# Attention scores as three fp32r passes over high and low parts, in a two-layer encoder kernel

## The reference

```python
q = partial_rope(_rms_f32(q, g_q), cos, sin) * (D_HD ** -0.5)
k = partial_rope(_rms_f32(k, g_k), cos, sin)
...
def block(qblk):                       # 128 queries
    s = jnp.einsum("bhcqd,bhckd->bhcqk", qblk, k)      # c: 2 components, d: 64
    p = jax.nn.softmax(s, axis=-1)
    a = p[:, :, 0] - lam * p[:, :, 1]
    return jnp.einsum("bhqk,bhkv->bhqv", a, v)
```

## Time and profile before

| | us |
|---|---|
| median of 3 runs | 1906.34 |
| lowest, highest | 1904.99, 1906.96 |
| the profiled execution | 1907.49 |
| its span, first to last instruction | 1905.7 |

### The profile page before, as it was taken

The page is one execution under the profiler, slowest core; times in us unless marked ns, Lnnn a source line. Parts: engine busy times, 40 slices in busy tenths (PEclk is TensorE's granted clock), DMA queues, the critical chain, the costliest instruction groups (busy, mean ns, idle before and its releaser), DMA issues.

```text
span 1905.7 us, 31585 instructions
## 1 busy us (share of the span) xinstructions
PE 1879.5 (99%) x10881; PEld 1750.2 (92%) x10881; DVE 1251.1 (66%) x2148; ACT 870.3 (46%) x1839; POOL 1159.5 (61%) x1533
## 2 busy tenths in 40 slices
PE   8999999999999999999999999999999999999999
PEld 7888887899999999999988888888889999999998
DVE  7756465677757665656776666666488575757673
ACT  5333333346444444444534444444465454544453
POOL 3533524357777868788863333333458787887885
PEclk9999999999999999999999999999999999999999
DMA  5559999527569898784366666655124435353534
GB/s 164 177 196 262 227 256 243 142 83 174 128 173 257 233 263 270 229 266 148 117 135 128 127 122 126 127 116 115 58 85 121 133 111 150 97 153 103 153 115 129
DMA packets 378986, 305.39 MB, mean 160 GB/s; under 512 B 14260, under 2 KB 322263, under 8 KB 378599
## 3 DMA queue, kind: packets, MB, share of 16 engines
q1 hardware_dynamic: 348304, 233.69, 40.3%
q0 software_dynamic: 28416, 69.21, 20.1%
q10 hardware_dynamic: 2134, 0.82, 0.2%
HBM read 298.88 MB, written 143.20 MB: 232 GB/s over the span
## 4 chain that ended last, share of the span: by engine, by line
PE 89%; DVE 6%; DMA 2%; ACT 1%; issue 1%; POOL 1%; DVEq 0%; SPq 0%; ACTq 0%; POOLq 0%
PE ps L929 48%; PE ps L836 26%; PE ps L1082 3%; PE ps L1243 3%; PE ps L1211 2%; PE ps L1062 1%; PE ps L1233 1%; PE ps L1145 1%; DMA raw<-in_sums 1%; DMA raw<-in_ffn_w_out_dram 1%; DVE gt L1586 1%; DVE rstd L1429 1%; PE ps L1091 1%; DVE sx L1481 0%; PE ps L1175 0%
## 5 line engine op out<-in xcount | busy, mean ns | idle before, releaser
L929 PE MATMUL ps<-sx,wh 128*128 128x400 f32 (+1 forms) x2044 | 532.3, 342 | 5.1 <-ACT gt L2163 4.2
L760 POOL TENSOR_TENSOR wl<-raw,wh 128x256 fp32r<-128x256 f32 (+1 forms) x432 | 356.4, 860 | 97.8 <-ACT wh L2148 96.5
L726 POOL CAST wh<-raw 128x256 fp32r<-128x256 f32 x248 | 102.2, 454 | 490.3 <-PE ps L836 466.5
L929 PEld LDWEIGHTS ps<-sx,wh 128*128 128x128 f32 x2044 | 374.5, 189 | 7.7 <-ACT gt L2163 5.3
L929 PE MATMUL ps<-sx,wl 128*128 128x400 f32 (+1 forms) x1022 | 348.5, 341 | 0.0
L760 POOL TENSOR_TENSOR wl<-raws,wh 128x256 fp32r<-128x256 f32 x328 | 282.3, 903 | 92.3 <-ACT wh L2148 92.0
L1640 DVE TENSOR_TENSOR h<-h,ps 128x400 f32<-128x400 f32 (+1 forms) x280 | 154.6, 559 | 131.9 <-PE ps L929 131.8
L929 PE MATMUL ps<-fx,wh 128*128 128x400 f32 (+1 forms) x904 | 235.2, 341 | 0.3 <-issue 0.2
L836 PE MATMUL ps<-xh,wh 128*128 128x512 f32 (+1 forms) x752 | 215.6, 363 | 0.0
L836 PE MATMUL ps<-xl,wh 128*128 128x512 f32 (+1 forms) x752 | 207.4, 349 | 0.0
L836 PE MATMUL ps<-xh,wl 128*128 128x512 f32 (+1 forms) x752 | 201.3, 345 | 0.0
(11 more groups left out here) (311 smaller groups left out, 3597.3 us busy)
## 6 DMA issues: line engine op xcount, KB each, us to landing
in_sums<-in_ffn_w_in_dram SPq DMA_DIRECT2D x16, 1536.0 KB, 9.3
raw<-in_sums SPq DMA_DIRECT2D x96, 256.0 KB, 3.1
in_sums<-in_ffn_w_in_dram SPq DMA_DIRECT2D x16, 1280.0 KB, 9.6
raw<-in_ffn_w_in_dram SPq DMA_DIRECT2D x80, 256.0 KB, 3.0
raws<-in_sums SPq DMA_DIRECT2D x80, 256.0 KB, 3.0
raw<-out_sums SPq DMA_DIRECT2D x120, 128.0 KB, 2.3
raws<-in_ffn_w_in_dram SPq DMA_DIRECT2D x52, 256.0 KB, 3.3
raw<-in_m_w_in_dram SPq DMA_DIRECT2D x24, 512.0 KB, 4.6
```

What stands on the lines that cost most here:

```text
L726: ins = pool.tensor_copy(wh[:, slot, c], raw[:, slot, c])
L760: ins = pool.tensor_tensor(slot_of(n, 1)[:, c], raw_of(n)[:, c], slot_of(n, 0)[:, c].bitcast(F32), ALU.subtract)
L929: mm = pe.matmul(product_bank(layer, s, j), slot_of(n, low_w)[:, k * P:(k + 1) * P], x, start=(j in OPENS and k + q == 0), stop=(k == tile ...
```

## The change

High and low parts of queries and keys are made, and each score matmul becomes three fp32r ones. The parts need room: the high rows lie in the four tiles of h that rest (`LATE`), which are stored to DRAM before attention and read back in the last head; the low rows lie over the first four rows of wk. `kd` becomes two, `kdh` and `kdl`.

```diff
+        def q_high(odd):
+            return high_rows[:, LATE[2 * odd], 0:TQ]
+        def k_high(odd):
+            return high_rows[:, LATE[2 * odd + 1], :]
+        def q_low(odd):
+            return low_rows[:, odd, 0:TQ]
+        def k_low(odd):
+            return low_rows[:, 2 + odd, :]
...
 SP, loads of the attention blocks n:
                 weights(MIX1 + n, n % 2, attn_cols(n % 3, (n // 3) * P))
+                if n == 1:
+                    sp.wait_ge(out_read, N_OUT)
+                    for odd in range(2):
+                        sp.dma_start(h_late[odd], h[:, LATE[2 * odd]:LATE[2 * odd] + 2, :]).then_inc(h_late_stored, 16)
+            def late_tiles_back(odd):
+                sp.wait_ge(sc_ready, (D_HEADS - 1 + odd) * NQ)
+                sp.wait_ge(h_late_stored, 32)
+                sp.dma_start(h[:, LATE[2 * odd]:LATE[2 * odd] + 2, :], h_late[odd]).then_inc(h_late_back[odd], 16)
...
 POOL:
+            def query_lows(g):
+                odd = g % 2
+                pool.wait_ge(q_high_ready, g + 1)
+                for c in pieces(TQ):
+                    ins = pool.tensor_tensor(q_low(odd)[:, c], wk[:, odd, c], q_high(odd)[:, c].bitcast(F32), ALU.subtract)
+                ins.then_inc(q_low_ready, 1)
...
+                if n > MIX1 + 2 and n % 3 == MIX1 % 3:
+                    query_lows((n - MIX1) // 3 - 1)
...
 TensorE, attn_scores:
                 if i == 0:
-                    pe.wait_ge(kn_ready, hd + 1)
+                    pe.wait_ge(q_low_ready, hd + 1)
+                    pe.wait_ge(kd_ready, 2 * hd + 2)
...
+                passes = ((q_high, k_high, kdh), (q_high, k_low, kdl), (q_low, k_high, kdh))
...
+                    for t, (query, _, block) in enumerate(passes):
+                        pe.matmul(between, query(odd)[:, q], block[:, odd, :], start=(t == 0), stop=(t == 2),
+                                  skip_group_check=True)
+                for t, (query, key, _) in enumerate(passes):
+                    for c in range(2):
+                        rows = slice(D_HD * c, D_HD * (c + 1))
+                        a, b = ((0, 512), (TAIL, keys))[c] if keys > 512 else (0, keys)
+                        mm = pe.matmul(both[:, c, a:b], query(odd)[rows, q], key(odd)[rows, START[s] + a:START[s] + b],
+                                       start=(t == 0), stop=(t == 2), skip_group_check=True)
...
 TensorE, head:
                 if first:
-                    keys_block(0, 3)
+                    keys_block(0, 2)
+                    attn_scores(hd, odd, 0, first=True)
+                    keys_block(2, 4)
                 attn_scores(hd, odd, 1)
...
                 turn_values(hd, n if not last else OUT1, 0)
-                beside(keys_block, 3 if first else 2, 4, (0, 2, 4))
+                if not first:
+                    beside(keys_block, 2, 4, (0, 2, 4))
                 turn_values(hd, n, 1)
...
+                beside(values_block, 5, 6, (3, 0, 3))
                 if not last:
                     attn_scores(hd + 1, even, 0)
                 if not first:
                     turn_output(hd - 1, even, 0)
-                beside(values_block, 5, 6, (3, 0, 3))
                 attend(hd, odd, 4)
...
 DVE:
+            def key_lows(g, odd, x):
+                for part, ready in enumerate((k_high_part, k_high_ready)):
+                    keys = K_PART[part]
+                    ve.wait_ge(ready, g * 2 + 2)
+                    v(ve.tensor_tensor(k_low(odd)[:, keys], x[:, keys], k_high(odd)[:, keys].bitcast(F32), ALU.subtract))
                 v.wait()
+                for rows, keys, at_col in KD_PART:
+                    ve.tensor_copy(kdl[rows, odd, at_col], k_low(odd)[rows, keys].bitcast(F32)).then_inc(kd_ready, 1)
...
-                combine(hd, 4)
                 if not last:
                     invert_key_roots(hd + 1, even)
                 maxima(hd, odd, 5)
+                combine(hd, 4)
                 if not last:
-                    normalise_k(hd + 1, even, kx, 0)
+                    normalise_k(hd + 1, kx, 0)
                 output(hd, odd, 3)
                 if not last:
                     invert_query_roots(hd + 1, even)
-                    normalise_k(hd + 1, even, kx, 1)
+                    normalise_k(hd + 1, kx, 1)
+                    key_lows(hd + 1, even, kx)
                 if not first:
                     scale_output(hd - 1, even)
...
 ACT:
+            def query_highs(g, odd):
+                sc.wait_ge(q_roped, g + 1)
+                sc.activation(q_high(odd), wk[:, odd, 0:TQ], ACT.Copy).then_inc(q_high_ready, 1)
+            def key_highs(g, odd, part):
+                sc.wait_ge((kn_part, kn_ready)[part], g + 1)
+                done, x = (k_high_part, k_high_ready)[part], wk[:, 2 + odd, :]
+                rows, keys, at_col = KD_PART[part]
+                sc.activation(k_high(odd)[:, K_PART[part]], x[:, K_PART[part]], ACT.Copy).then_inc(done, 1)
+                sc.activation(kdh[rows, odd, at_col], x[rows, keys], ACT.Copy).then_inc(done, 1)
...
                 turned(hd, 3)
+                if not last:
+                    query_highs(hd + 1, even)
                 exps(hd, odd, 5)
+                if not last:
+                    key_highs(hd + 1, even, 0)
                 squared(hd, odd, 3)
+                if not last:
+                    key_highs(hd + 1, even, 1)
```

78 lines of the change are left out of this document (46 added, 32 removed).

## The result

| | before | after |
|---|---|---|
| median, us | 1906.38 (4 runs) | 1920.58 (4 runs) |
| lowest, highest | 1904.99, 1906.96 | 1919.61, 1921.93 |
| the profiled execution, its span | 1907.49, 1905.7 | 1920.29, 1918.5 |

The changed kernel is slower: the ratio is 1.0077, with a 95% interval from 1.0064 to 1.0089. That is 14.2 us where the prediction had 7.6. The direction held, and so did the stated range of 1905 to 1922 us, but nearly half of the loss was not in the sum, and 1920.6 lies outside what the prediction calls the case's own range, 1910 to 1918.

A forecast was written before the change was run, and what follows sets the result against it. TensorE, busy 45.9 of 46 us, was taken as the bound. Losses of 7.1, 2.75, 0.1 and 1.55 less savings of 3.2 and 0.7 gave +7.6 us, counted from the 1906.34 median: 1914.0 us, range 1905 to 1922.

The forecast's parts named there:

- rival A: Score matmuls: the fixed 0.206 us belongs to each pair, not the group; 4.9 us more, 1919; chance 0.13.
- D: Output turn of part 1: the gap doesn't open because DVE's chain ends earlier than its rows say; 1906.9 us; chance 0.10.
- The gap at the turn of part 1: End of six heads: TensorE waits 1.46 us instead of 0.28 because a values step moved away; 7.1 us lost.
- The last head, 1.55: Last head: filler moved ahead of the turn of part 0, so part 1 starts later; 1.55 us lost.
- The moves as a whole: TensorE's reordering in steady heads, first head, its end and last head: losses of 11.5 us.
- The score matmuls: Attention scores: three fp32r passes, halves side by side, save 0.067 us a block over 48 blocks; 3.2 us saved.
- B: Score matmuls: fp32r halves don't run side by side; 28 us more, 1942; chance 0.09.
- C: Score matmuls: fp32r avoids the fixed 0.206 us and the switch; 20.6 us saved in place of 3.2, 1896.6; chance 0.07.
- The keys' wait: TensorE's wait for the keys' first part shrinks as DVE loses two small products; 0.7 us saved (0 to 1.2).
- the 0.15 above: Steady heads' low parts: cover is gone if DVE comes 0.15 us late; every further 0.1 us costs six times 0.1.
- The first head: First head: later second scores lose 1.7 us, an uncovered wait for ACT's copy 1.0; 2.75 us lost.
- The stores of h: Four tiles of h leave in two DMAs of 800 KB before attention and come back in the last head; priced at nothing.

The follow-up runs named there:

- experiment 1: The kernel before, fp32 scores kept, with only TensorE's order changed as the change does it: 1916.98 us, ratio 1.0062.
- experiment 4: The changed kernel with values steps shifted by one (5 before the scores, 6 behind the turn of part 0) and the last head's filler behind the turn again: 1918.44 us.
- experiment 3: The changed kernel with POOL's low parts of the queries held until DVE has combined query block 4: 1918.77 us, ratio 1.0068.
- experiment 6: The changed kernel with the two stores of h two places later on SP's queue, behind the fourth block of weights: 1919.43 us, ratio 1.0068.
- experiment 9: The changed kernel with shifted steps, later POOL low parts, stores after small loads, first head rearranged, ACT copying values before second exponentials: 1906.96 us, ratio 1.0002.
- experiment 10: The kernel of experiment 9 with h's stores two places later on SP and POOL's weight split held in the first head: 1904.97 us, ratio 0.9993.
- experiment 5: The changed kernel with SP issuing the stores of h only after the small lambda loads have landed: 1920.41 us, ratio 1.0067.

## Why the prediction was right, and where it was wrong

**The range: held by luck.** It reached up to 1922 us to take in rival A, which is dead, and down to 1905 for D, which is dead too. By its own terms, 1910 to 1918, the measured 1920.6 is outside. The forecast's mechanism, a loss by the moves that fp32r's saving doesn't cover, is what happened; the rest is below, term by term.

**The gap at the turn of part 1, six times 1.18: right.** DVE's chain takes what it took in the earlier trace rows, the wait list has 1.2 each (D is dead), and experiment 1 has it in fp32 as well. The head itself grows by 1.07 there, since at its new place the step costs some 0.1 us less around it (in experiment 1 1.43 us from the turn of attention 4 to the scores, where 0.32 without the step and 1.18 for it make 1.50).

**The last head, 1.55: right.** Part 0 is turned at 1369.17, part 1 at 1371.42, 2.25 us later, with the filler now ahead of both, other than in the earlier trace rows; experiment 4, with the filler behind the turn, gives 1.5 us back.

**The moves as a whole: right.** Their terms (7.1, 2.75, 0.1 and 1.55) make 11.5 us; experiment 1 measured 10.6 by the medians, 10.95 against the runs beside it, 10.8 from the first mark on. The first head has 2.8 of it, as forecast.

**The score matmuls: the mechanism right, the size off.** The fixed part is paid once in a group (A is dead), the halves overlap (B is dead), and fp32r pays the switch too (C is dead). The halves save 0.84 us a head (5.56 to 4.72 us in all from start to start), and 0.80 was forecast. But the short matmul costs 0.14 more and not 0.10, 0.38 us in the mean where it was 0.24: it takes 0.33 behind a block step and 0.42 to 0.44 behind other work. So a head saves 0.28 us in place of 0.40, and eight save 2.2 in place of 3.2.

**The keys' wait: the step that failed.** The prediction has "I take 0.7" saved, by comparing instructions that leave DVE (two products) and come earlier (the combining of block 4). The combining was priced at its duration before the change. At that duration the keys are just in time, as experiment 3 shows: 1.54 us between the two turns where the kernel before has 1.75, which would have been 1.2 us saved in six heads, the upper end of what the prediction allowed. But beside POOL's new subtractions it takes 0.77 us more, all of which TensorE waits: 2.30 us between the turns, 0.55 more than before the change, 3.3 us in six heads, where -0.7 stood. The prediction did name the danger, "If POOL's run slows DVE, that is the 0.15 above", but put it at the low parts, where the step covers it, and not one place ahead of them. I had looked at what POOL's instructions wait for and not at what runs on DVE in the same 2.1 us. The Trainium skill ("SBUF — State Buffer", SBUF: two separate sides) has the rule that I should have weighed: DVE and GpSimd share a pair of ports under an exclusive lock, which a DVE instruction in a two-port mode needs, and one with two SBUF inputs against a GpSimd instruction that reads SBUF; whichever starts first keeps it for its whole length. The trace mostly agrees: both instructions of `combine` have two SBUF inputs and lengthen, those that read PSUM don't, and in the first head of the changed kernel, where DVE's low part starts first (981.58, 0.68 us, its plain length), it is POOL's piece from 981.61 that takes 1.24 us in place of 0.73. But the second (0.95 us, from 1072.22) is done 0.3 us after POOL's last piece ends at 1072.88, less than its own 0.50 behind a lock held to that end.

**The first head: mostly right, with two terms missing.** Beside the 2.8 us of the moves it lost another 1.1: 0.6 that experiment 6 has as well, and 0.5 that go with the fall of the clock. POOL's split beside the low parts costs a wait of 0.95 to 0.99 us (experiments 6 and 9, gone in 10). In the changed kernel's own profile this wait does not show, since the clock fell there, and the slow matmuls reach over it. Windows of 2 us, the granted clock is the third number from the end:

```profile
980.00:982.00 2.00, 0.43 (x3) 0.34 (x3) 1.87 (x4) 1.40 (x5) 1.92 (x6) 0.99 1.07 191
982.00:984.00 2.00, 2.00 (x7) 1.98 (x7) 1.93 (x4) 0.66 (x1) 2.00 (x3) 0.50 0.87 164
984.00:986.00 2.00, 2.00 (x11) 1.96 (x10) 0.47 (x1) 0.00 (x0) 2.00 (x3) 0.65 0.09 15
986.00:988.00 2.00, 2.00 (x13) 1.59 (x14) 1.10 (x1) 0.00 (x0) 0.31 (x1) 1.00 0.83 232
```

TensorE idled for 1.57 us from about 980.2; then the clock is 0.50, the 1.2 GHz level, and twelve matmuls take 3.84 us, from 981.72 to 985.56, where experiment 1 has 2.31 for the same twelve at 1.00. These are 1.5 us, but against experiment 6, which has the wait of 0.95 in its place, the scores start 0.5 us later behind the second turn of key roots (6.0 and 5.5 us).

**The stores of h: priced at nothing, not quite nothing.** I checked what stands behind them on SP's queue, and not what else was in flight on the transfer engines: four loads of 32 KB on ACT's queue, which DVE reads at once. Their delay is shown; its cost in the median is about 1 us by experiment 6 and not certain, and the changed kernel's own profile has nothing of it (first mark at 978.0, 978.3 before the change).

**The sum again.** From the first mark to the end of the program the two profiled executions take 927.4 and 940.5 us, 13.1 apart. The terms give 13.2: the moves 10.8, the keys' wait 3.3, the first head 1.1 (POOL beside the low parts and the clock, less what its scores save), the scores of the other seven heads -2.0. The medians are 14.2 apart. The 1.1 us left over fit the stores, but the changed kernel's own profile doesn't have them, so this term rests on the medians of 4 and 5 runs. Of the prediction's miss of 6.6 us, 4.0 is the keys' wait, 1.0 the score matmuls, 1.4 the first head (1.1 and the 0.3 that its scores save) and about 1 the stores, less 0.6 to 0.9 that the moves cost less.

**Where the change could go.** With the waits away (experiment 10) the kernel is at 0.9993 of the one before. How much of that is the format is not shown: no run has the remedies with fp32 scores, and they also take away the 0.2 us a head by which the kernel before turned its key roots late. By the score matmuls' own pace the faster format is worth 2.2 us here, and everything that prepares it must be hidden entirely for that to show.

## What to carry to other kernels

Before you give an idle engine new work, look at what its neighbour runs in the same microseconds: POOL's free time was real, and yet its work doubled short DVE instructions that stood ahead of TensorE. When a step of filler is moved to hide a new chain, write down the chain that it hid before; it will come back whole, and taking one wait away only pays in full when the next engine in line (here ACT's order) is looked at as well. Changes of format and changes of order should be run apart: here the order alone made three quarters of the loss.

## What I had not expected of the hardware

- DVE instructions on SBUF data beside a running POOL subtraction or split: 0.22 to 0.54 us (one column), 0.50 to 0.95 (272 columns), 1.16 to 1.77 or 2.09 (two of 512 and 288), 0.37 to 1.27 (two of 16). Reciprocals keep theirs (0.17 us for 128x2 at 1071.45 in the changed kernel, beside POOL). Instructions that read PSUM keep their length beside POOL: 0.69 for the product on the keys' first part and 0.99 for the evacuation, both in the first head of experiments 5 and 9, as in the earlier trace rows and elsewhere.
- Two halves of the array take their matmuls from the program's order independently: three of one half written ahead of three of the other cost 0.90 us, alternating ones 0.89.
- fp32r matmuls on 64 rows keep the pace of the full array, though each needs new weights on rows that were just in use: 0.22 us from the second pass of 512 columns to the third (1077.71 to 1077.93), 0.213 of it the columns at 2.4 GHz. The Trainium skill ("TensorE: Matmul & The Clock Gate", What overlaps and what doesn't) lets a load of weights overlap a running matmul only when the row group differs; by that each further pass would show its load, and this row does not.
- The clock falls after an idle time in some cases and not in others of the same length. After 1.57 us at the same place it fell to 0.50 in the changed kernel and stayed at 1.00 in experiment 4, where it fell 10 us later, behind idle times of 0.84 and 0.75; in experiment 1 three of 1.70, 0.85 and 0.75 left it at 1.00.
- Two stores of 800 KB issued on SP's queue among four loads of 32 KB on ACT's put off the last of these: it landed 7.5 to 9.4 us after its issue in the six profiles with the stores there, and 3.6 to 4.1 us after it in the seven without.
